# VectorE takes the mean and reciprocal of the memory's rows before the mixes of two narrow products, and scales those rows after the last operand sum of the receptance product

## The reference

```python
def _rms_norm(x, g):
    y = xf * lax.rsqrt(jnp.mean(xf * xf, axis=-1, keepdims=True) + NORM_EPS)
    return (y * g.astype(jnp.float32)).astype(x.dtype)

# time mixing on the normed rows h of layer 0
dx = h_prev - h
xr, xw, xk, xv, xa, xg = [h + dx * mix[i] for i in range(N_MIX)]
r = xr @ wr                      # the receptance: 1024 x 1024
k = xk @ wk
v = xv @ wv
w_log = -softplus(-(w0 + tanh(xw @ w1) @ w2)) - 0.5    # w1: 1024 x 64
a = sigmoid(a0 + (xa @ a1) @ a2)                       # a1: 1024 x 64
g = sigmoid(xg @ g1) @ g2                              # g1: 1024 x 128
...
# keys and values of the memory, once for both layers
mem_kv = _rms_norm(mem, norm_mem) @ xa_wkv             # mem: 256 x 1024
```

## Time and profile before

| what | value |
|---|---|
| median of 3 runs | 1718.11 us (1712.77 to 1719.11) |
| the profiled execution's own time | 1720.79 us |
| its span, first to last instruction | 1719.0 us |
| mean granted TensorE clock over the span | 0.954 of full |
| TensorE busy | 1532.1 us, 89% |
| VectorE busy | 830.9 us, 48% |
| ScalarE busy | 420.9 us, 24% |
| GpSimd busy | 162.5 us, 9% |
| DMA, mean over the span | 183 GB/s |

### The profile page before, as it was taken

How to read it: one execution, slowest core, us unless ns; L and a number is a source line. 1 busy time by engine, 2 the same in 40 slices (tenths; PEclk the granted TensorE clock), 3 DMA queues, 4 the chain that set the end, 5 groups by cost and what they waited for, 6 DMA issues and landing times.

```text
span 1719.0 us, 28891 instructions
## 1 busy us (share of the span) xinstructions
PE 1532.1 (89%) x12461; PEld 950.5 (55%) x12461; DVE 830.9 (48%) x1416; ACT 420.9 (24%) x849; POOL 162.5 (9%) x181
## 2 busy tenths in 40 slices
PE   6899968888999999879878899999999997988886
PEld 4777757777654774534333368746558544333332
DVE  6474866554465535534231264446643544431225
ACT  2124225555400221401000120117421322100002
POOL 2000113322000000011110200000000001110101
PEclk9899979999999999979998999999999996998999
DMA  8116400002441611379999942220024025999995
GB/s 271 41 57 221 141 3 4 4 10 71 146 149 49 245 50 53 146 274 418 424 425 425 365 151 98 98 98 1 2 108 186 7 108 187 386 423 424 424 417 220
DMA packets 82337, 315.03 MB, mean 183 GB/s; under 512 B 17968, under 2 KB 19048, under 8 KB 57312
## 3 DMA queue, kind: packets, MB, share of 16 engines
q1 hardware_dynamic: 70112, 284.86, 42.6%
q0 software_dynamic: 10944, 24.10, 3.8%
q10 hardware_dynamic: 1152, 4.19, 0.6%
HBM read 306.86 MB, written 34.34 MB: 198 GB/s over the span
## 4 chain that ended last, share of the span: by engine, by line
PE 78%; DVE 9%; issue 6%; ACT 4%; DMA 2%; POOL 0%; PEld 0%; POOLq 0%; DVEq 0%; SPq 0%; ACTq 0%
PE PS L774 17%; PE PS L2615 14%; PE PS L641 12%; PE PS L1360 9%; PE PS L2640 6%; PE PS L1736 2%; PE PS L1672 2%; PE PS L2600 2%; PE PS L612 2%; DVE arena L1052 2%; PE PS L1712 1%; PE PS L1992 1%; PE PS L2013 1%; PE PS L537 1%; PE PS L2003 1%
## 5 line engine op out<-in xcount | busy, mean ns | idle before, releaser
L774 PE MATMUL PS<-arena,ring 128*128 128x256 f32 x1344 | 297.6, 382 | 3.9 <-DVE arena L895 2.9
L774 PEld LDWEIGHTS PS<-arena,ring 128*128 128x128 f32 x1344 | 256.1, 192 | 42.4 <-issue 5.8
L2615 PE MATMUL PS<-ring,arena 128*64 128x512 f32 x512 | 134.3, 685 | 54.3 <-issue 51.3
L641 PE MATMUL PS<-ring,arena 128*128 128x512 f32 x400 | 178.7, 593 | 0.7 <-ACT arena L1958 0.7
L2623 DVE TENSOR_TENSOR arena<-PS,arena 128x256 f32<-128x256 f32 x32 | 13.6, 424 | 252.3 <-PE PS L2630 233.1
L2615 PE MATMUL PS<-arena 128*64 128x512 f32 x512 | 117.2, 611 | 12.3 <-issue 9.5
L2615 PEld LDWEIGHTS PS<-ring,arena 128*64 128x64 f32 x512 | 44.3, 157 | 142.5 <-issue 139.1
L641 PEld LDWEIGHTS PS<-ring,arena 128*128 128x128 f32 x400 | 74.3, 191 | 83.3 <-issue 82.3
L2620 ACT ACTIVATE arena<-PS 128x256 f32<-128x256 f32 x32 | 12.3, 383 | 358.9 <-PE PS L2615 358.9
L813 DVE TENSOR_TENSOR arena<-arena,PS 128x512 f32<-128x512 f32 x56 | 36.8, 683 | 108.7 <-PE PS L774 108.7
L2615 PEld LDWEIGHTS PS<-arena 128*64 128x64 f32 x512 | 40.9, 141 | 86.9 <-issue 83.3
(11 more groups left out here) (331 smaller groups left out, 2290.3 us busy)
## 6 DMA issues: line engine op xcount, KB each, us to landing
arena<-in_moe_w SPq DMA_DIRECT2D x96, 1024.0 KB, 15.9
ring<-in_moe_w SPq DMA_DIRECT2D x96, 1024.0 KB, 14.1
ring<-in_sb_wqkv SPq DMA_DIRECT2D x6, 2048.0 KB, 10.3
ring<-in_xa_wq SPq DMA_DIRECT2D x4, 2048.0 KB, 8.4
ring<-in_xa_wo SPq DMA_DIRECT2D x4, 2048.0 KB, 14.2
ring<-in_xa_wkv SPq DMA_DIRECT2D x3, 2048.0 KB, 10.6
h<-in_x SPq DMA_DIRECT2D x8, 512.0 KB, 8.5
ring<-in_rw_wr SPq DMA_DIRECT2D x2, 2048.0 KB, 11.4
```

What stands on the lines that cost most here:

```text
L641: ins = pe.matmul(PS[:, BANK_OF[g], :], rows(k), cols[:, k, :], start=(k == 0 and not grows), stop=(k == 3), skip_group_check=grows)
L774: ins = pe.matmul(PS[:, BANK_OF[g], M * c:M * c + M], rows[:, k, o:o + P], cols[:, k, :], start=(c + k == 0 and not grows), stop=(k == 3), ...
L2615: ins = pe.matmul(bank(2, 2, F)[r, :, :], xgT[p][:, k, r], w[a][:, :, k, :], start=(k == 0), stop=(k == KC - 1))
```

## The change

`norm_vec` is cut in two: `row_scales` (mean and reciprocal) and a new `scale_rows` (the scaling). For the receptance's stage VectorE's order becomes: the first seven sums and two adds, `row_scales` of the memory, the mixes of w1 and a1, the last sum, the scaling of the memory's two tiles, the last adds. No instruction is added or removed, no other engine's program changes, and the other users of `norm_vec` keep their order.

```diff
         def norm_vec(vec, name, src, tn):
             row_scales(vec, name)
+            scale_rows(vec, name, src, tn)
+
+        def scale_rows(vec, name, src, tn):
             for t in range(dict(NORMS)[name]):
                 vec.tensor_scalar(tn[:, t, :], src[:, t, :], rstd[:, t:t + 1], None, ALU.mult)\
                     .then_inc(S("norm_rows"), 1)
@@
             mix(0, *MIXES[0])
             left_sums(vec, "wr", RK_S1)
             sums_T(vec, "wr", xm[1], RK_S1, RK_TS["wr"], R_)
+            row_scales(vec, "mem")
             mix(1, *MIXES[1])
             mix(2, *MIXES[2])
-            norm_vec(vec, "mem", mem_rows, mem_tn)
             last_sum(vec, "wr", xm[1], RK_TS["wr"])
+            scale_rows(vec, "mem", mem_rows, mem_tn)
             last_adds(vec, "wr", R_)
             mix(3, *MIXES[3])
             mix(4, *MIXES[4])
```

## The result

The changed kernel takes 1703.27 us, median of 5 runs (1699.38 to 1708.41), against 1718.11 us, also of 5 runs, for the kernel before: a ratio of 0.992, 95% interval 0.9893 to 0.9948. That is 14.8 us less between the medians, where 10.1 were forecast, and inside the range given. The profiled execution took 1704.77 us, its span 1703.0.

A forecast was written before the change was run, and what follows sets the result against it. TensorE was taken as the bound, at 78% of the chain. Its wait of 7.55 us plus 2.6 us of clock gave 10.1 us, taking the median from 1718.11 to 1708.0 us, range 1702 to 1715.

The forecast's parts named there:

- theory B: Experiments' theory: everything behind the receptance's stage gains another 4 to 5 us once it starts earlier; no chance given.
- The wait of 7.55 us goes: Receptance's stage, before group 6: TensorE's idle 7.55 us vanishes, with 2.8 us to spare.
- The clock gives back 2.6 us: Groups 6 and 7 of the receptance run at the full clock without the pause, gaining 2.6 us.
- The first rival: The clock gives nothing back, or its loss turns up at the next pause: gain 7.55, 1710.5 us; chance 0.17.
- The estimate from the Trainium skill: Clock term for groups 6 and 7 between 1.1 us and the whole 2.6, the sum 8.7 to 10.1.
- The bound of 3.0 us from above: Clock term's upper bound, from groups 0 to 5 taking 23.77 us against 20.8 at the stage's other cold start.
- The last sum's move is worth nothing: VectorE's last sum ahead of the scaling gains nothing; group 10, which needs it, leaves 5.4 us to spare.
- The mixes and the scaling move for free, everything behind follows: Mixes have 20 us to spare, scaling 35; groups 8 to 13, loads and later stages come 10 us earlier.
- The rival of a loss on the way: After 76.2 us, other engines or transfers absorb half or more of the gain: 1713 to 1718 us; chance 0.15.
- the slower one: Pairs' stage, started at another moment, granted 1.2 GHz for part of its work: 1727 us; chance 0.03.

The follow-up runs named there:

- the run against itself: The kernel before, unchanged, timed against itself: 1715.97 us against 1717.44, ratio 0.9981.
- once more: The changed kernel without further edit, timed again beside the kernel before: 1705.54 us against 1717.44, ratio 0.9942.
- first half: Changed kernel with the memory's scaling put back ahead of the last sum; mean and reciprocal stay ahead of the mixes: 1704.46 us against 1717.44 before, ratio 0.992.
- root later: Kernel before with ScalarE's root of the memory moved behind its copies of groups 4, 5 and 6, VectorE untouched: 1706.16 us against 1717.44, ratio 0.9933.
- 4 mixes: Changed kernel with mean and reciprocal behind 4 of the 16 mixes: 1702.42 us against 1716.53 for the kernel before, ratio 0.9922.
- 8 mixes: Changed kernel with mean and reciprocal behind 8 of the 16 mixes: 1707.72 us against 1716.53 for the kernel before, ratio 0.995.
- 12 mixes: Changed kernel with mean and reciprocal behind 12 of the 16 mixes: 1711.30 us against 1716.53 for the kernel before, ratio 0.9979.
- second half: Changed kernel with mean and reciprocal put back behind the 16 mixes, last sum still ahead of the scaling: 1714.81 us against 1716.53 before, ratio 0.9997.
- work inside the wait: Kernel before with 16 unread TensorE matmuls added between groups 5 and 6 of the receptance: 1715.16 us against 1715.46, ratio 0.9994.
- 8 more mixes: Kernel before with the 8 mix instructions of w1 made twice: 1720.58 us against 1715.46, ratio 1.0033.
- the doses: Changed kernel with mean and reciprocal behind 4, 8 and 12 of the 16 mixes: 1702.42, 1707.72 and 1711.30 us against 1716.53 for the kernel before.

## Why the prediction was right, and where its size was off

**Where the time went.** One number per profile says when the stage ends: the start of TensorE's first work behind group 13, a turn of `prow` that stands 0.2 us ahead of the products of w1 and a1. Beside it the mean of all runs of each kernel (for the kernel before, the 72 runs beside the others, without the 12 of the run against itself; for the five kernels without a TensorE wait, 33):

| kernel | TensorE's wait, us | groups 6 and 7, us | work behind group 13 starts at, us | mean time, us |
|---|---|---|---|---|
| changed, once more, first half, root later, 4 mixes | 0 | 6.91 | 74.6 to 75.8, mean 75.2 | 1705.1 |
| 8 mixes | 2.25 | 7.01 | 77.7 | 1707.5 |
| 12 mixes | 5.04 | 8.66 | 81.6 | 1711.9 |
| before (two profiles) | 7.55 | 9.51, 9.31 | 86.3, 86.0 | 1716.5 |
| second half | 7.54 | 9.11 | 85.1 | 1715.5 |
| work inside the wait | 0.64 | 7.01 | 83.6 | 1714.8 |
| 8 more mixes | 12.97 | 9.60 | 90.7 | 1720.6 |

From the first row to the last the stage grows by 15.5 us and the time by 15.5. In between it is 2.5 for 2.4, 6.4 for 6.8, and for the kernel before 11.0 (the mean of its two profiles, 86.14, less 75.17) for 11.4. What the stage loses or gains goes through to the end about one for one.

The profiles say it without the spread of the runs. TensorE's first work of the pairs' stage comes at 227.27 us in the kernel before and at 216.72 in the changed one, 140.95 us behind that milestone in both, and 140.9 to 141.0 in all twelve profiles: up to there nothing is lost or added. From the milestone to the end of the span it is 1626.6 us in the mean of the five profiles without a wait (1624.5 to 1629.5) and 1626.2 in the mean of the seven others (1621.8 to 1632.7). No extra 4 us come with the earlier start: **theory B falls**.

The forecast's sum of 10.1 us stands against 11.4 (standard error about 0.8, from a spread of 4 us a run) over these runs. The choice of runs matters by as much: with the 12 runs of the kernel before against itself it is 11.2, and with each of the five kernels set against the runs beside it, 12.2. The 14.8 between the first medians of five lies above all of these.

**Where the spread is.** The profiled spans of before and after differed by 5.4 us beyond the stage. Some 2 of these come in the pairs' stage, some 3 behind it. Windows of all engines over the pairs' stage (length; busy time and count of PE, PEld, DVE, ACT, POOL; TensorE's clock, DMA share, GB/s), the kernel before in its two profiles:

```profile
227.30:452.40 225.10, 197.14 (x6756) 168.26 (x6758) 119.73 (x196) 111.26 (x176) 60.18 (x42) 0.96 0.07 18
```

```profile
226.90:442.80 215.90, 190.26 (x6754) 162.84 (x6756) 118.98 (x196) 111.30 (x176) 60.38 (x42) 0.99 0.07 19
```

The same work takes 225.1 and 215.9 us in the same kernel, at a mean clock of 0.96 and 0.99, and 223.1 and 218.2 in the changed kernel's two profiles, at 0.97 and 0.99. The clock does not account for all of it: the stage takes 218.5 us at 0.97 in the kernel with the later root and 221.7 at 0.99 in that of the first half. Over all twelve profiles it is 215.4 to 225.1, in either order of VectorE. One profile against one can't settle 5 us here.

**The steps, one by one.**
- *The wait of 7.55 us goes*: right, with slack as forecast; the doses show it in fine steps, and the kernel with the later root shows the way it took.
- *The clock gives back 2.6 us*: right. The full stall costs 2.2 to 2.6 us in three profiles, and work inside the wait takes the cost away though ScalarE and VectorE are as late as before. The first rival, that it gives nothing back, falls. The estimate from the Trainium skill ("TensorE: Matmul & The Clock Gate", Part 1: The HAM clock gate), 1.1 to 2.6, holds these values; that the cost differs between executions of one kernel is seen here too, but by less: 2.60 and 2.40 us in the two profiles of the kernel before.
- *The bound of 3.0 us from above* was ill founded. It took all that groups 0 to 5 lie over 20.8 us for the clock. In the changed kernel they took 23.36 us (48.05 - 24.69) with a granted clock of 1.00 recorded over all of it, and in the kernel behind 4 mixes 22.71, with 0.58 recorded from 24.6 to 28 us and 0.92 from there to 31.5. What stretches the start of the stage is not only the recorded clock. The forecast's reason for the term, that the clock was at 1.00 as long as TensorE was busy, also holds only from 31.5 us on: from 24.6 to 28 and from there to 31.5 the kernel before has 0.50 and 0.66 recorded with TensorE busy. For groups 6 and 7 it came out.
- *The last sum's move is worth nothing*: right, in both directions (first half alone, second half alone).
- *The mixes and the scaling move for free, everything behind follows*: right. SyncE's two loads of the ring went out at 68.97 and 75.87 instead of the earlier trace rows, the memory's first turn came at 93.41 (93.9 forecast), and what the stage gave was kept to the end, within the spread. The rival of a loss on the way falls, as does the slower one.
- *The size*: 10.1 forecast, 10.55 in the stage in the first pair of profiles (0.40 of it lies ahead of group 6, 48.05 against 48.45, where the change touches nothing; 10.15 is the wait and the clock), 11.2 to 12.2 over all runs, depending on which are compared. What remains above 10.1 is not separated from spread. If a term of the sum was too small it is by 1 to 2 us, and no run here names one. That the first medians stood 14.8 us apart, well inside the range but half as much again as forecast, is within the spread of five runs against five, and no support for the sum's size.

No version beats the changed kernel clearly: the five kernels without a wait have medians from 1702.4 to 1706.2 us, and their intervals overlap.

## What to carry to other kernels

Follow a stall of the bounding engine through every queue on the way: here a 0.16 us instruction of VectorE stood behind 10.6 us of work that nobody needed yet, and reached TensorE only because ScalarE's root stood ahead of a copy that frees a bank. Either queue can be mended, the small instruction earlier or the copies ahead of the waiting root, and the slack (here 2.8 us) says how exact the place must be. Add to a TensorE stall what its clock costs after it, but only for a pause that is long enough to lower it; and when a few microseconds are in question, compare the milestones of the stage in several profiles, not two spans.

## What the runs showed of the hardware

- The price of a TensorE pause beyond its own length, read from two groups that take 6.91 us at the full clock: 0.1 us after 2.25 us idle (and the same 0.1 after 0.64), 1.75 after 5.04, 2.2 to 2.6 after 7.5, 2.7 after 12.97. It rises, and from 7.5 us on hardly more.
- Matmuls can be slow with a recorded clock of 1.00. In the changed kernel, from 24.6 us on, TensorE's windows show 1.00 while the matmuls there have a median of 634 ns, against 379 later in the stage:

```profile
L777 PE MATMUL PS<-arena,ring x20: 379/634/767, 24.7 to 31.4; 128*128 128x256 f32 x20
```

```profile
24.60:28.00 3.40, 3.31 (x8) 1.00 1.00 305
28.00:31.50 3.50, 3.50 (x14) 1.00 1.05 390
```

The same median of 634 stands in the first profile of the kernel before with a recorded clock of 0.50 and 0.66. The arriving mixes (8 in 5.38 us) and the loads (DMA share 1.0) don't explain it alone: both are the same in the kernel behind 4 mixes, where the median of this stretch is 379 and groups 0 to 5 take 0.65 us less. Whether the record misses a change of the clock was not tried.
